# Hymba step on one Trainium2 core: the last head pair's keys and values stored from SBUF

## The chip, the cores and the metric

The kernel runs on one core of one Trainium2 chip. The metric is the device time of one execution in microseconds (us). In what follows PE is the matrix engine, DVE the vector engine, ACT the scalar engine, POOL is GpSimd and SP the engine that here only issues DMAs. ACT issues DMAs too. "The SP queue" and "the ACT queue" are the two DMA queues; in the profile they are q1 and q10.

## What is computed

One layer of a decoder, for 512 prompt tokens and 8 samples of 8 new tokens, with a cache of 2048 keys and values per sample:

```python
proj = jnp.einsum('btd,de->bte', x, w_in)                 # 1024 -> 4096
q, k, v, g_att, gb, gc, hh, g_conv = jnp.split(proj, ...)
o_att = _dilated_attention(q, k_all, v_all, offset)       # windows (128,1) (512,4) (2048,16)
att = o_att * jax.nn.silu(g_att)
u = gc * hh                                               # width-3 causal convolution of u
z = gb * y_conv * jax.nn.silu(g_conv)
out = jnp.einsum('bte,ed->btd', jnp.concatenate([att, z], axis=-1), w_out)
y = _layer_norm(DEEPNORM_ALPHA * x + out, ln_g, ln_b)
new_k = k_all[:, n_all - keep:]                           # the whole cache is an output again
new_v = v_all[:, n_all - keep:]
```

The last two lines matter here: the caches of keys and values are read, and nearly all of them must be written again as outputs. The host splits each cache into a part that the dilated windows use ("used") and one that they don't ("rest").

## The kernel before

All tensors are float32. Products of the two projections are made of three passes over a high and a low part of each operand (`x_hi`, `x_lo`, `w_hi`, `w_lo`). ACT makes a high part by a rounding copy, DVE the low part by a subtraction.

The input projection works through 32 weight tiles of 128 columns. Each tile from 2 on is loaded by SP into one of two slots of `w_raw` (512 KB, `load_w`, L311), rounded by ACT (`split_hi`, L510), subtracted by DVE (`split_lo`, L847) and multiplied by PE in two halves (`project`, L1239 to L1241, banks `pj_a` and `pj_b`). The tiles are taken in four rounds, one for a pair of heads; tiles 27 to 31 belong to the last round (`act_last_round`, `dve_last_round`, `pe_last_round`). Round by round the attention of a head pair stands between the projections: for the samples PE reads the used keys from `k_buf` in four pieces (L1402, `sample_scores`) and the used values from `v_buf` in ten half pieces, which are loaded two at a time (L1436, `sample_values`).

SP loads in a written order: weight tiles, four key pieces of 1280 KB per pair (L318, semaphores `k_in`), five value loads of 1024 KB per pair (L325, `v_in`). At the end it loads eight tiles of `w_out` into `wo_raw` (512 KB each, `load_wo`, L392). `wo_raw` lies over `k_buf` and other early buffers, so that the first four wait for `k_used`, PE's count of key pieces that it has read. ACT rounds them in `split_wo` (L689) and DVE subtracts (L1013). Later SP loads `ln_gb` (L428) and the residual rows `x_res` (L438), which lie over `v_buf` from the second tile of rows on.

The used and rest parts of the caches go to their outputs by 57 copies from HBM to HBM, each issued by ACT wherever `copy_next` stands in its written program (L539 rest, L548 values, L543 keys; 1024 KB, keys 1280 KB). Their order is: 24 copies of the rest, 17 of values, 16 of keys. Three more pieces of values (numbers 2, 3, 4 of the last pair, `STORED`) are stored from `v_buf` by SP (`store_values`, L420). All copies count on one semaphore, `copied`, and the three stores on `v_stored`; SP waits for both totals as its last act.

Behind the input projection stand the output projection (L1561 to L1595, five tiles of tokens) and the layer norm on DVE (L1186 to L1230). The last tile's rows are stored by SP (L458) and ACT (L837) in halves.

What an engine's program holds is executed in its order: a DMA whose semaphore isn't there yet holds up all that stands behind it on SP or on ACT.

Of the kernel before, what the change touches and what calls it, by code (L numbers as in the profile page):

```python
# [7 lines left out]
P = 128  # L8
# [21 lines left out]
NPAIR = DEC_BATCH // 2  # L30
# [11 lines left out]
K_PIECES = 4  # L42
# [3 lines left out]
V_LOADS = V_PIECES // 2  # L46
STORED = (2, 3, 4)
N_COPIES = 2 * REST_ROWS + NPAIR * (K_PIECES + V_LOADS) - len(STORED)
QT = SEQ // P
# [44 lines left out]
def layer_step(nc, d):  # L94

    with ExitStack() as ctx:
# [6 lines left out]
        def sem(name):  # L103
            return ctx.enter_context(nc.semaphore(name))
# [66 lines left out]
            sem("k_saved"), sem("v_saved"), sem("vn_saved"), sem("copied"), sem("conv_out"))  # L171
        v_stored = sem("v_stored")
        y_out = [sem(f"y_out{n}") for n in range(Y_SLOTS)]
# [132 lines left out]
        def _(sp):  # L306
# [88 lines left out]
            pieces = K_PIECES * (NPAIR - 1)  # L395
            sp.wait_ge(k_used, pieces + 1)
            load_wo(0)
            load_v(NPAIR - 1, 2)
            load_w(W_TILES - 1)
            sp.wait_ge(k_used, pieces + 2)  # L400
            load_wo(1)
            load_v(NPAIR - 1, 3)
            sp.wait_ge(k_used, pieces + 3)
            load_wo(2)
            load_v(NPAIR - 1, 4)
            sp.wait_ge(k_used, pieces + 4)
            load_wo(3)
            load_wo(4)
# [8 lines left out]
            def store_values(m):  # L417
                n = V_LOADS * (NPAIR - 1) + m
                sp.wait_ge(v_in[m], 16 * NPAIR)
                sp.dma_start(d["v_used_out"][n * P:(n + 1) * P, :], v_buf[:, m * 2048:(m + 1) * 2048])\  # L420
                    .then_inc(v_stored, 16)

            store_values(2)


# [10 lines left out]
            def load_res(t):  # L436
                rows = P if t != SAMPLE_AT else NS
                sp.dma_start(x_res[0:rows, t * 1024:(t + 1) * 1024], d["x_rows"][y_rows(t), :]).then_inc(res_in[t], 16)  # L438

# [23 lines left out]
            sp.wait_ge(copied, 16 * N_COPIES)  # L463
            sp.wait_ge(v_stored, 16 * len(STORED))

# [35 lines left out]
        def _(act):  # L501
# [44 lines left out]
            def copy_v(i, s):  # L546
                rows = slice((V_LOADS * i + s) * P, (V_LOADS * i + s + 1) * P)
                act.dma_start(short_runs(d["v_used_out"][rows, :]), short_runs(d["v_used"][rows, :]))\  # L548
                    .then_inc(copied, 16)

            copies = iter(range(N_COPIES))

            def copy_next():

                n = next(copies)
                if n < 2 * REST_ROWS:
                    copy_rest(n)
                elif n < N_COPIES - NPAIR * K_PIECES:
                    n -= 2 * REST_ROWS
                    copy_v(n // (V_LOADS), n % (V_LOADS))  # L560
                else:
                    n -= N_COPIES - NPAIR * K_PIECES
                    copy_k(n // K_PIECES, n % K_PIECES)
# [147 lines left out]
            def act_round(i):  # L711
# [42 lines left out]
                copy_q(i + 1)  # L754
                copy_next()
                split_hi(t0 + 8)
# [5 lines left out]
                split_k(i + 1, 1)  # L762
                copy_next()
                split_hi(t0 + 9)
                out_sample(i)

            def act_last_round(i):
                t0 = tile0(i)
                copy_c(i, 0)
                copy_next()  # L770
                out_sample_turned(i - 1)
                exp_prompt(i, 0)
                copy_c(i, 1)
                move_prompt(i, 0)
                exp_prompt(i, 1)
                split_hi(t0 + 2)
                move_prompt(i, 1)
# [31 lines left out]
                copy_next()  # L809
                copy_next()  # L810
                split_mix(2)
                copy_next()
                copy_next()
# [10 lines left out]
            for t in range(QT + 1):  # L824
# [7 lines left out]
                nc.scalar.activation(std[0:rows, :], rstd[0:rows, :], ACT.Sqrt).then_inc(ln_sqrt, 1)  # L832
                if t < 3:
                    copy_next()
# [882 lines left out]
```

## Time and profile before

| | us |
|---|---|
| median of 3 runs | 355.65 |
| the 3 runs | 355.65, 355.94, 352.95 |
| the profiled execution's own time | 352.72 |
| its span, first to last instruction | 350.9 |
| PE busy | 341.5 (97%) |
| DVE busy | 207.4 (59%) |
| ACT busy | 122.9 (35%) |
| DMA, mean rate | 402 GB/s over 141.03 MB |

The profile is of one execution. Its own time is 1.8 us above its span, and 2.9 us below the median of the runs. Idle time of an engine is read with what ended it; a DMA has a row at its issue and a time from there to its landing.

### The profile page before, as it was taken

To read this page: it belongs to the slowest core of one execution; us is meant where nothing else is said; L and a number is where in the kernel's file an instruction comes from. 1 tells how busy PE (TensorE), PEld (TensorE's weight loads), DVE (VectorE), ACT (ScalarE), POOL (GpSimd) and SP (SyncE) were. 2 spreads that over 40 slices of the span, in tenths; PEclk is the share of its full clock that TensorE was granted. 3 is DMA by queue.
4 is the path that set the end of the run, shared out by engine and by line. 5 is a ranking of instruction groups with operands and counts; after the bars stand their busy time and mean duration, and the time that the engine had idled before them with its cause. 6 is when DMAs were issued, how large, how long until landed. Compare 5 with 4: busy or idle time off the path is not lost.

```text
span 350.9 us, 7296 instructions
## 1 busy us (share of the span) xinstructions
PE 341.5 (97%) x3048; PEld 298.4 (85%) x3048; DVE 207.4 (59%) x397; ACT 122.9 (35%) x249; POOL 11.4 (3%) x28
## 2 busy tenths in 40 slices
PE   8999999999999999999999999999999999999991
PEld 6998888998889889988898899888889887888791
DVE  3744518955254657652546486524546699794874
ACT  5634324342244333422442425224442744310100
POOL 0010000000100000001000000010000000200000
PEclk9999999999999999999999999999999999999997
DMA  8999999999999999999999999999999999999995
GB/s 293 401 423 424 408 422 419 421 423 420 420 418 420 424 421 418 378 420 418 416 417 423 419 418 365 420 403 419 424 422 417 419 410 339 378 400 391 406 356 221
DMA packets 31570, 141.03 MB, mean 402 GB/s; under 512 B 3121, under 2 KB 3505, under 8 KB 26545
## 3 DMA queue, kind: packets, MB, share of 16 engines
q1 hardware_dynamic: 15890, 76.34, 53.4%
q10 hardware_dynamic: 15648, 64.23, 46.3%
q8 instruction: 24, 0.39, 0.4%
q14 instruction: 8, 0.07, 0.0%
HBM read 132.66 MB, written 71.86 MB: 583 GB/s over the span
## 4 chain that ended last, share of the span: by engine, by line
PE 81%; DMA 9%; DVE 6%; ACT 2%; issue 1%; ACTq 0%; DVEq 0%
PE pj_b L1239 9%; DMA w_raw<-in_w_tiles 9%; PE pj_b L1241 8%; PE pj_b L1240 8%; PE pj_a L1239 7%; PE pj_a L1240 6%; PE pj_a L1241 6%; PE sc L1436 4%; PE sc L1402 4%; PE px L1593 3%; PE px L1595 3%; PE px L1594 3%; PE po L1382 2%; PE pt L1368 2%; PE px L1350 2%; DVE rg L974 1%
## 5 line engine op out<-in xcount | busy, mean ns | idle before, releaser
L1239 PE MATMUL pj_b<-x_hi,w_hi 128*128 128x320 f32 x248 | 78.5, 316 | 0.3 <-DVE mix L990 0.3
L1240 PE MATMUL pj_b<-x_lo,w_hi 128*128 128x320 f32 x248 | 76.5, 308 | 0.0
L1241 PE MATMUL pj_b<-x_hi,w_lo 128*128 128x320 f32 x248 | 76.5, 308 | 0.0
L1239 PE MATMUL pj_a<-x_hi,w_hi 128*128 128x256 f32 (+1 forms) x248 | 71.6, 289 | 0.0
L1241 PE MATMUL pj_a<-x_hi,w_lo 128*128 128x256 f32 (+1 forms) x248 | 69.4, 280 | 0.0
L1240 PE MATMUL pj_a<-x_lo,w_hi 128*128 128x256 f32 (+1 forms) x248 | 69.4, 280 | 0.0
L847 DVE TENSOR_TENSOR w_lo<-w_raw,w_hi 128x1024 fp32r<-128x1024 f32 x30 | 36.7, 1223 | 27.5 <-ACT w_hi L510 27.5
L1239 PEld LDWEIGHTS pj_a<-x_hi,w_hi 128*128 128x128 f32 x248 | 46.9, 189 | 6.1 <-issue 5.5
L1239 PEld LDWEIGHTS pj_b<-x_hi,w_hi 128*128 128x128 f32 x248 | 46.5, 188 | 4.8 <-issue 3.6
L510 ACT CAST w_hi<-w_raw 128x1024 fp32r<-128x1024 f32 x30 | 31.4, 1045 | 46.0 <-PE pj_b L1241 28.6
L1241 PEld LDWEIGHTS pj_a<-x_hi,w_lo 128*128 128x128 f32 x248 | 46.7, 188 | 0.0
L1240 PEld LDWEIGHTS pj_a<-x_lo,w_hi 128*128 128x128 f32 x248 | 46.6, 188 | 0.0
L1240 PEld LDWEIGHTS pj_b<-x_lo,w_hi 128*128 128x128 f32 x248 | 46.5, 188 | 0.0
L1241 PEld LDWEIGHTS pj_b<-x_hi,w_lo 128*128 128x128 f32 x248 | 46.5, 188 | 0.0
L974 DVE RECIPROCAL rg<-rg 128x256 f32<-128x256 f32 (+1 forms) x16 | 31.3, 1954 | 0.6
L636 ACT ACTIVATE p_pr<-p_pr,stat 128x512 f32<-128x512 f32 (+3 forms) x32 | 17.7, 553 | 12.5 <-DVE stat L936 12.5
L1402 PE MATMUL sc<-k_buf,q_bd 128*32 128x320 f32 x256 | 20.3, 435 | 0.4 <-DVE stat L961 0.4
L936 DVE CUSTOM_DVE_ANT_0 p_pr<-px,mask_pr 128x512 f32<-128x512 f32 (+3 forms) x32 | 14.1, 487 | 9.7 <-PE px L1350 9.7
L1436 PE MATMUL sc<-v_buf,pt_s 128*32 128x256 f32 x320 | 19.3, 382 | 0.0
L642 ACT COPY pt_pr<-pt 128x384 f32<-128x384 f32 (+1 forms) x24 | 11.2, 517 | 15.3 <-PE pt L1368 15.3
L1436 PEld LDWEIGHTS sc<-v_buf,pt_s 128*32 128x32 f32 x320 | 9.4, 109 | 7.0 <-issue 1.8
L899 DVE COPY qk<-pj_b 128x320 f32<-128x320 f32 x4 | 2.0, 492 | 22.0 <-PE pj_b L1241 22.0
(175 smaller groups left out, 470.3 us busy)
## 6 DMA issues: line engine op xcount, KB each, us to landing
k_buf<-in_k_used SPq DMA_DIRECT2D x16, 1280.0 KB, 13.5
v_buf<-in_v_used SPq DMA_DIRECT2D x20, 1024.0 KB, 14.9
out_k_used_out<-in_k_used ACTq DMA_DIRECT2D x16, 1280.0 KB, 20.9
out_v_used_out<-in_v_used ACTq DMA_DIRECT2D x17, 1024.0 KB, 15.9
w_raw<-in_w_tiles SPq DMA_DIRECT2D x30, 512.0 KB, 9.7
out_k_rest_out<-in_k_rest ACTq DMA_DIRECT2D x12, 1024.0 KB, 14.6
out_v_rest_out<-in_v_rest ACTq DMA_DIRECT2D x12, 1024.0 KB, 16.4
wo_raw<-in_w_out SPq DMA_DIRECT2D x8, 512.0 KB, 13.7
```

What stands on the lines that cost most here:

```text
L510: nc.scalar.copy(w_hi[:, c], w_raw[:, c]).then_inc(w_hi_done, 1)
L636: nc.scalar.activation(p, p, ACT.Exp, bias=negmax_pr[:, st:st + 1], scale=-1.0, accum_out=sum_pr[:, st:st + 1]).then_inc(pr_exp, 1)
L642: nc.scalar.copy(pt_pr[:, e * SEQ:e * SEQ + step_width(s)], pt[e][:, 0:step_width(s)])\
L847: nc.vector.tensor_tensor(w_lo[:, c], w_raw[:, c], w_hi[:, c].bitcast(F32), ALU.subtract)\
L936: nc.vector.tensor_tensor_reduce(out=p_pr[:, e * SEQ + c0:e * SEQ + c1], in0=px[e][:, c0:c1], in1=mask_pr[:, SEQ - width(u):], scale=-SCAL ...
L974: nc.vector.reciprocal(rg[:, c], rg[:, c]).then_inc(g_step, 1)
L1239: nc.tensor.matmul(out, w_hi[:, w], x_hi[:, c], start=(k == 0), stop=False)
L1240: nc.tensor.matmul(out, w_hi[:, w], x_lo[:, c], start=False, stop=False)
L1241: return nc.tensor.matmul(out, w_lo[:, w], x_hi[:, c], start=False, stop=(k == KT - 1))
L1402: last = nc.tensor.matmul(sc[r * 32:r * 32 + 32, 0:K_COLS], q, k_buf[:, k0:k0 + K_COLS], start=(b == 0), stop=(b == 1 and not ends), skip_ ...
L1436: last = nc.tensor.matmul(sc[r * 32:r * 32 + 32, 0:2 * P], pt_s[:, t * P + r * 32:t * P + r * 32 + 32], v_buf[:, v0:v0 + 2 * P], start=(t ...
L1593: nc.tensor.matmul(out, m_hi, wo[:, hi], start=(n == 0), stop=False)
```

## The change

Every piece of the last pair's used keys and values now goes out from SBUF, where it lies anyway for the attention. Four stores of keys (`store_k`, 1280 KB each, from `k_buf`) are issued by ACT, each behind a wait that the piece has landed (`k_in`). Five stores of values, two of them new, are issued by SP. Six copies go: the four of those keys and the two of those values. The copies are 51 now. One call of `copy_next` is added early in the last round, two are taken out late in it, and two behind the layer norm's square roots; two calls in the third round and one at the start of the last become stores.

The single counts of stores are now one semaphore each. SP waits for `k_stored[c]` ahead of each of the loads of `w_out` that lie over the key piece, and for `v_stored[0]` or `v_stored[1]` ahead of the residual rows 1 to 4.

```diff
-STORED = (2, 3, 4)
-N_COPIES = 2 * REST_ROWS + NPAIR * (K_PIECES + V_LOADS) - len(STORED)
+N_COPIES = 2 * REST_ROWS + (NPAIR - 1) * (K_PIECES + V_LOADS)
...
+            sp.wait_ge(k_stored[0], 16)
             load_wo(0)
...
+            sp.wait_ge(k_stored[1], 16)
             load_wo(1)
...
+            sp.wait_ge(k_stored[2], 16)
             load_wo(2)
             load_v(NPAIR - 1, 4)
             sp.wait_ge(k_used, pieces + 4)
+            sp.wait_ge(k_stored[3], 16)
             load_wo(3)
...
+            store_values(0)
             store_values(2)
+            store_values(1)
...
             def load_res(t):
                 rows = P if t != SAMPLE_AT else NS
+                if t:
+                    sp.wait_ge(v_stored[(t - 1) // 2], 16)
...
+            def store_k(c):
+                n = K_PIECES * (NPAIR - 1) + c
+                act.wait_ge(k_in[c], 16 * NPAIR)
+                act.dma_start(d["k_used_out"][n * P:(n + 1) * P, :], k_buf[:, c * K_SLOT:(c + 1) * K_SLOT])\
+                    .then_inc(k_stored[c], 16)
...
             def act_last_round(i):
                 t0 = tile0(i)
                 copy_c(i, 0)
-                copy_next()
+                store_k(2)
                 out_sample_turned(i - 1)
                 exp_prompt(i, 0)
                 copy_c(i, 1)
+                copy_next()
                 move_prompt(i, 0)
                 exp_prompt(i, 1)
+                store_k(3)
                 split_hi(t0 + 2)
...
                 out_sample(i)
                 copy_next()
-                copy_next()
                 split_mix(2)
-                copy_next()
                 copy_next()
...
-                if t < 3:
+                if t < 1:
                     copy_next()
```

On ACT, at the turn from the third round to the last, these stood in a row before (`w_hi` is a weight tile's high part, `gcs` and `p_pr` are the convolution's gate and the prompt's scores):

```order
L543 DMA out_k_used_out<-in_k_used 16x16x1280
L685 COPY att_s<-pt 64x64 [waits so_turned]
L685 COPY att_s<-pt 64x64
L636 ACTIVATE p_pr,stat<-p_pr,stat 128x512 [waits pr_masked] x2
L649 COPY gcs<-pj_b 128x320 [waits vt_done,pj_b_done]
L642 COPY pt_pr<-pt 128x512 [waits pr_turned] x2
L636 ACTIVATE p_pr,stat<-p_pr,stat 128x384 [waits pr_masked] x2
L510 CAST w_hi<-w_raw 128x1024 [waits pj_b_done,w_in1]
```

and these stand there now:

```order
L563 DMA out_k_used_out<-k_buf 128x2560 [waits k_in2]
L700 COPY att_s<-pt 64x64 [waits so_turned]
L700 COPY att_s<-pt 64x64
L651 ACTIVATE p_pr,stat<-p_pr,stat 128x512 [waits pr_masked] x2
L664 COPY gcs<-pj_b 128x320 [waits vt_done,pj_b_done]
L552 DMA out_k_used_out<-in_k_used 16x16x1280
L657 COPY pt_pr<-pt 128x512 [waits pr_turned] x2
L651 ACTIVATE p_pr,stat<-p_pr,stat 128x384 [waits pr_masked] x2
L563 DMA out_k_used_out<-k_buf 128x2560 [waits k_in3]
L519 CAST w_hi<-w_raw 128x1024 [waits pj_b_done,w_in1]
```

The one copy has become a store of key piece 2, and two more DMAs of 1280 KB stand ahead of the tile's rounding: a copy, and the store of piece 3.

On SP, in the last round (`wo_raw` are the tiles of `w_out`), the difference is:

```order
-L392 DMA wo_raw<-in_w_out 128x1024 [waits k_used]
+L392 DMA wo_raw<-in_w_out 128x1024 [waits k_stored0,k_used]
 L325 DMA v_buf<-in_v_used 128x2048 [waits v_used]
 L311 DMA w_raw<-in_w_tiles 128x1024 [waits w_lo_done]
-L392 DMA wo_raw<-in_w_out 128x1024 [waits k_used]
+L392 DMA wo_raw<-in_w_out 128x1024 [waits k_stored1,k_used]
 L325 DMA v_buf<-in_v_used 128x2048 [waits v_used]
-L392 DMA wo_raw<-in_w_out 128x1024 [waits k_used]
+L392 DMA wo_raw<-in_w_out 128x1024 [waits k_stored2,k_used]
 L325 DMA v_buf<-in_v_used 128x2048 [waits v_used]
-L392 DMA wo_raw<-in_w_out 128x1024 [waits k_used]
+L392 DMA wo_raw<-in_w_out 128x1024 [waits k_stored3,k_used]
```

The loads stand where they stood; four of them have a second wait. The load of the last weight tile (L311) stands between the first and the second of these.

## Rows read from the trace of the kernel before

**Rows 1.** The page's first part and the rate of its 40 slices.
```profile
PE 341.5 (97%) x3048; PEld 298.4 (85%) x3048; DVE 207.4 (59%) x397; ACT 122.9 (35%) x249; POOL 11.4 (3%) x28
...
GB/s 293 401 423 424 408 422 419 421 423 420 420 418 420 424 421 418 378 420 418 416 417 423 419 418 365 420 403 419 424 422 417 419 410 339 378 400 391 406 356 221
```

**Rows 2.** Engines by stretch; last three: PE clock, DMA share, GB/s.
```profile
240.00:256.00 16.00, 16.00 (x166) 13.27 (x167) 8.81 (x24) 8.38 (x20) 0.00 (x0) 1.00 1.02 423
...
272.00:288.00 16.00, 15.74 (x145) 13.40 (x144) 12.67 (x18) 10.00 (x16) 0.00 (x0) 1.00 1.02 419
288.00:296.00 8.00, 8.00 (x76) 5.95 (x75) 7.93 (x9) 4.38 (x6) 0.00 (x0) 1.00 1.02 347
```

**Rows 3.** Timeline of ACT: start, us, instruction, idle before and releaser.
```profile
251.87 1.03 ACT L510 CAST w_hi<-w_raw 128x1024 fp32r<-128x1024 f32 x1
...
271.69 1.05 ACT L510 CAST w_hi<-w_raw 128x1024 fp32r<-128x1024 f32 x1 [5.03 <-PE pj_b L1241]
...
281.13 1.05 ACT L689 CAST wo<-wo_raw 128x1024 fp32r<-128x1024 f32 x1
...
284.22 0.38 ACT L654 ACTIVATE rg<-pj_a 128x256 f32<-128x256 f32 x1 [2.04 <-PE pj_a L1241]
...
291.72 1.05 ACT L689 CAST wo<-wo_raw 128x1024 fp32r<-128x1024 f32 x1
```

**Rows 4.** The chain that ended last, 270 to 292 us: start, us, what.
```profile
272.52 0.59 ACTq L543
...
274.20 1.89 ACT wo L689 x2
...
282.05 2.17 DVE rg L974
...
285.44 0.41 PE pj_b L1239
```

**Rows 5.** Timeline of SP: issues of the last weight tile and of a w_out tile.
```profile
254.19 0.33 SPq L311 DMA_DIRECT2D w_raw<-in_w_tiles  x1
...
264.21 5.07 SPq L392 DMA_DIRECT2D wo_raw<-in_w_out  x5
```

**Rows 6.** DMA issues, 254.1 to 254.5 us: KB, us to landing.
```profile
w_raw<-in_w_tiles SPq DMA_DIRECT2D x1, 512.0 KB, 10.0
```

**Rows 7.** DMA queues, 256 to 262 us: packets, MB, share of 16 engines.
```profile
q1 hardware_dynamic: 490, 2.47, 99.6%
...
q10 hardware_dynamic: 7, 0.02, 0.8%
```

**Rows 8.** DMA queues, 276 to 284 us.
```profile
q10 hardware_dynamic: 352, 1.72, 51.7%
q1 hardware_dynamic: 377, 1.67, 50.6%
```

**Rows 9.** DMA issues, 232.9 to 233.3 us (key piece 3).
```profile
k_buf<-in_k_used SPq DMA_DIRECT2D x1, 1280.0 KB, 14.3
```

**Rows 10.** DMA issues, 242.3 to 242.95 us (a key copy).
```profile
out_k_used_out<-in_k_used ACTq DMA_DIRECT2D x1, 1280.0 KB, 15.3
```

**Rows 11.** DMA issues, 264.2 to 264.5 us (w_out tile 3).
```profile
wo_raw<-in_w_out SPq DMA_DIRECT2D x1, 512.0 KB, 11.8
```

**Rows 12.** DMA issues, 268.85 to 269.2 us (w_out tile 7).
```profile
wo_raw<-in_w_out SPq DMA_DIRECT2D x1, 512.0 KB, 17.9
```

**Rows 13.** DMA issues, 292.5 to 292.8 us (residual rows 0).
```profile
x_res<-in_x_rows SPq DMA_DIRECT2D x1, 512.0 KB, 12.3
```

**Rows 14.** Timeline of DVE: the layer norm's first residual sum, and a wait later.
```profile
307.14 0.68 DVE L1186 SCALAR_TENSOR_TENSOR y_t<-x_res,px 128x512 f32<-128x512 f32 x1
...
325.08 0.69 DVE L1186 SCALAR_TENSOR_TENSOR y_t<-x_res,px 128x512 f32<-128x512 f32 x1 [4.00 <-PE px L1595]
```

**Rows 15.** DMA issues, 326.9 to 327.2 us (the last key copy, issued at 326.97).
```profile
out_k_used_out<-in_k_used ACTq DMA_DIRECT2D x1, 1280.0 KB, 22.2
```

**Rows 16.** DMA issues, 347.7 to 348 us (half of the last rows, issued at 347.76).
```profile
out_y<-y_t ACTq DMA_DIRECT2D x1, 256.0 KB, 2.7
```

More of the change, by code:

```diff
@@ L171, in layer_step @@
             sem("k_saved"), sem("v_saved"), sem("vn_saved"), sem("copied"), sem("conv_out"))
-        v_stored = sem("v_stored")
+        v_stored = [sem(f"v_stored{m}") for m in range(V_LOADS)]
+        k_stored = [sem(f"k_stored{c}") for c in range(K_PIECES)]
         y_out = [sem(f"y_out{n}") for n in range(Y_SLOTS)]
@@ L420, in store_values @@
                 sp.dma_start(d["v_used_out"][n * P:(n + 1) * P, :], v_buf[:, m * 2048:(m + 1) * 2048])\
-                    .then_inc(v_stored, 16)
+                    .then_inc(v_stored[m], 16)
+            store_values(0)
             store_values(2)
+            store_values(1)
             sp.wait_ge(s_pv, NPAIR)
@@ L463, in _ @@
             sp.wait_ge(copied, 16 * N_COPIES)
-            sp.wait_ge(v_stored, 16 * len(STORED))
+            for m in range(V_LOADS):
+                sp.wait_ge(v_stored[m], 16)
         @block.gpsimd
@@ L557, in copy_next @@
                     copy_rest(n)
-                elif n < N_COPIES - NPAIR * K_PIECES:
+                elif n < N_COPIES - (NPAIR - 1) * K_PIECES:
                     n -= 2 * REST_ROWS
@@ L561, in copy_next @@
                 else:
-                    n -= N_COPIES - NPAIR * K_PIECES
+                    n -= N_COPIES - (NPAIR - 1) * K_PIECES
                     copy_k(n // K_PIECES, n % K_PIECES)
@@ L754, in act_round @@
                 copy_q(i + 1)
-                copy_next()
+                if i < NPAIR - 2:
+                    copy_next()
+                else:
+                    store_k(0)
                 split_hi(t0 + 8)
@@ L762, in act_round @@
                 split_k(i + 1, 1)
-                copy_next()
+                if i < NPAIR - 2:
+                    copy_next()
+                else:
+                    store_k(1)
                 split_hi(t0 + 9)
@@ L773, in act_last_round @@
                 copy_c(i, 1)
+                copy_next()
                 move_prompt(i, 0)
                 exp_prompt(i, 1)
+                store_k(3)
                 split_hi(t0 + 2)
@@ L809, in act_last_round @@
                 copy_next()
-                copy_next()
                 split_mix(2)
-                copy_next()
                 copy_next()
```

## The prediction

> **What bounds the kernel now.** I read the page's first part first: PE is busy for 341.5 of 350.9 us [rows 1]. What is left is the start and the layer norm of the last tile, so a change can gain only there, and it loses whatever it makes PE wait. The clock was full (1.00) in all the stretches of [rows 2]. The rate of the 40 slices comes next: from the second slice on it stands near 420 GB/s [rows 1], and the table by stretch puts the DMA engines' share at 1.02 [rows 2]. So the DMA engines are full too, and a byte that is moved earlier on one queue makes a byte later on the other. That is the side from which this change is to be judged: it removes no work from PE, DVE or ACT.
>
> Then I looked for the loads that PE comes to need soonest. The last weight tile (31) is issued at 254.19 us [rows 5] and takes 10.0 us [rows 6], so it lands at 264.2. ACT rounds it at 271.69 and had been waiting for PE, not for the load [rows 3]: 7.5 us of slack. The chain that ended last says why that instruction matters. In the other rounds it runs along PE; from 272 to 285 us it runs over ACT (the queue's issue, two roundings of `w_out` from 274.20) and DVE (the gate's reciprocal until 284.2) to PE at 285.44 [rows 4]. An instruction of ACT that comes late at 271.69 delays all of this one for one, since nothing on that chain waits for anything else.
>
> **The change, part by part.** *Bytes.* A copy and a store move the same bytes through the DMA engines. In the stretch from 256 to 262 us the SP queue had them almost alone, with 2.47 MB in 6 us, or 412 GB/s [rows 7]; shared, they move 419 to 423 [rows 2]. I take 0.42 MB a us. Swapping a copy for a store of the same piece costs nothing by itself. What counts is when each is issued.
>
> *What ACT now issues ahead of the last weight tile.* Before, from 226.7 us until that tile landed, ACT issued three copies of values (1.05 MB each) and one of keys (1.31 MB). Now it issues, at the same places, stores of keys 0, 1 and 2 for the first, third and fourth, and then two more DMAs of 1.31 MB at about 249 and 252 us: a copy, and the store of keys 3, which stands just ahead of the rounding at 251.87 [rows 3]. The sum of what is added is 2 x 0.26 + 2 x 1.31 = 3.1 MB, which at 0.42 is 7.5 us. All of it is issued before the tile, and both queues have work, so all of it goes ahead of the tile or beside it. [Rows 7] show that it isn't filling a hole: the ACT queue had nothing left from 256 to 262 us, and the SP queue used the whole rate for these very loads.
>
> There is an echo. ACT's next copy is issued at 262.17 us, after which the tile needed 2 us only. A tile that is still 7.5 us off meets that copy, and where both queues have work they take turns packet by packet (352 to 377 packets in 8 us [rows 8]). So up to 1.31 MB more, 3.1 us, goes ahead. The tile lands between 264.2 + 7.5 = 271.7 and 264.2 + 10.6 = 274.8 us. Against 271.69 it is between 0.0 and 3.1 us late. I take 3.1, since the turns are nearly even and the copy's packets fit into the 7.5 us. If the ACT queue's larger packets (10 KB for a key store, 4 KB for a weight tile) give it more than its bytes, the tile comes still later; the price of this is bounded by one more of ACT's 1.31 MB, 3.1 us, so the term is 0 to 6.2, taken at **3.1 us**.
>
> *The tiles of `w_out`.* Each is behind the same bytes. Tile 3 is issued at 264.21 [rows 5] and lands 11.8 us later [rows 11], at 276.0; ACT takes it at 281.13 [rows 3]. By 10.6 us later it lands at 286.6, while ACT now wants it at 281.13 + 3.1 = 284.2. Its rounding takes 1.05 us, so it ends at 287.7. Behind it stands the gate's exponential of 284.22 [rows 3], now due at 287.3: 0.4 us late. Tile 7, issued at 268.85, lands 17.9 us later [rows 12] at 286.8, now at 297.4, wanted at 291.72 + 3.1 = 294.8 [rows 3]; DVE subtracts four of these in a row from there, and the last is needed some 3.5 us after ACT begins it, which hides it. Together **0.5 us**; from 0, if the echo is small, to 4, if every one of these is met by another copy of ACT.
>
> *The new waits on SP.* Key stores 0, 1 and 2 are issued at about 226.7, 240.1 and 242.4 us. The copy that stood at 242.4 took 15.3 us [rows 10]; by that the stores are there at 242, 255.4 and 257.7, against 244.75, 254.6 and 257.7 for the loads that wait. Store 3 is issued at 252 and is there at 267 to 268, so that tile 3 of `w_out` is issued some 3.5 us after 264.21, and tiles 4 to 7, queued behind it, follow. The SP queue still has older loads in it until 274 us, so this costs 0; without that cover it would be 3.5 us on tile 3, within the 4 above.
>
> *The new waits on ACT.* Key piece 3 was issued at 233.00 us and took 14.3 [rows 9], so it landed at 247.3; its store stands at 251.9, 4.6 us later, and behind it on ACT a weight tile's rounding. The pieces before have 4 us or more. The added bytes ahead of it are 0.26 MB, 0.6 us. Cost 0; up to 1 if a large store is just ahead.
>
> *Residual rows.* Two more stores of values, 2.1 MB or 5.0 us, are on SP ahead of `ln_gb` and `x_res`. Rows 0 landed at 292.5 + 12.3 = 304.8 [rows 13] and DVE took them at 307.14 [rows 14]. Behind tile 7 at 297.4 come three stores of 1.05 MB, at half the rate 15 us at most, so rows 0 land at 312 to 315 against 307.14 + 3.6 = 310.7: 1 to 4 us late. DVE waits 4.00 us for PE at 325.08 [rows 14], so it catches up. Cost 0, up to 3 if PE has to wait for the two sums.
>
> *The end.* The last key copy was issued at 326.97 and landed 22.2 us later, at 349.2 [rows 15]. The last rows of y landed at 347.76 + 2.7 = 350.5 [rows 16]. So in this execution the copies set nothing, and two fewer behind the layer norm gain 0. What they may gain in others is the second rival.
>
> **Sum.** 3.1 + 0.5 = 3.6 us on the profiled execution's own 352.72, which gives 356.3. That execution is 2.9 us under the median of the runs, 355.65, and nearest to the third of them. Carried to the median it is 355.65 + 3.6 = **359.3 us**. Its own range is 355.7 (both terms 0) to 362.3 (6.2 and 0.5).
>
> **The rivals.** *The tile is in time.* If the echo is small, it lands at 271.7 and ACT loses nothing: 355.6 us. For it: the margin is 7.5 us and the sum of bytes 7.5. Against it: the sum has no slack, and [rows 7] show no idle engine to take the bytes.
>
> *The end gets shorter.* Two of the three runs took 2.9 us more than the profiled one. If these are executions in which the copies landed after the last rows of y, then fewer copies at the end bring them back. For it: copies that run alone are slow. From 288 to 296 us the rate was 347 GB/s at the same share of 1.02 [rows 2], against 419 in the stretch before, so that a key copy alone costs 1.31 / 0.347 = 3.8 us in place of 3.1, and a store reads no HBM. Against it: the profile shows the last copy 1.3 us ahead of the end. It gives 355.65 - 2.9 = 352.7, less some tenths: 352.3 us. The Trainium skill has a rule for this ("HBM Reference", Specifications): a domain gives about 716 GB/s, reads and writes together being what a copy asks of it. By that rule a lone copy would run at half of 716, 358 GB/s, and the trace's 347 agrees. [...]
>
> *The loads starve.* If each late load lets more of ACT's copies pass, the tiles of `w_out` and the residual rows come late in turn: 6.2 for the weight tile and 2 for the rest, so 355.65 + 8.2 = 363.9 us. It decides once tile 31 lands more than 4 us after 271.69. Against it: while ACT waits it issues no copies, and the SP queue catches up.
>
> **Chances.** The forecast 0.40, the tile in time 0.24, the shorter end 0.19, the starved loads 0.17. About 1% (3.6 us) is what a measurement of this kernel can tell from no change. The forecast lies just at that line: I give 0.26 of its 0.40 to slower and 0.14 to the same. The starved loads are slower. Of the shorter end 0.12 is faster and 0.07 the same; the tile in time is the same. That makes faster 0.12, same 0.45, slower 0.43. The range goes from 352.6 to 363.9 us and leaves out about half of each outer case.
>
> **What would show it.** In the new trace the last `w_raw` load should take about 20 us to land in place of 10.0; ACT's rounding of tile 31 should wait for that DMA at 272 to 275 us, in place of waiting for PE; PE should show a wait of 1 to 3 us between 272 and 290. `w_out` tile 3 should land near 287. The copies should be done several us before the last rows of y. The prediction is wrong if the tile lands by 271.7, or if it lands late and PE doesn't wait, or if the copies turn out to have set the end.

## Result, and the profile after the change

The changed kernel is slower: 361.70 us, median of 4 runs (359.84 to 363.76), against 355.00 (352.95 to 355.94, 4 runs) for the kernel before. The ratio is 1.0182, with a 95% interval of 1.0135 to 1.0229. The profiled execution took 360.69 us, span 358.9, against 352.72 and 350.9.

The page of the changed kernel: busy time, the clock and the rate in 40 slices, and the bytes of HBM.

```profile
PE 344.0 (96%) x3048; PEld 299.7 (84%) x3048; DVE 208.2 (58%) x397; ACT 122.9 (34%) x249; POOL 13.1 (4%) x28
...
PEclk9999999999999999999999999999999999998998
...
GB/s 296 401 423 416 407 423 420 420 420 420 420 421 422 424 419 397 386 423 415 406 425 420 422 384 385 422 414 428 418 414 423 421 420 426 400 401 384 398 77 58
...
HBM read 125.32 MB, written 71.86 MB: 549 GB/s over the span
```

Against [rows 1], PE is busy only 2.5 us longer, in a span longer by 8.0. The reads of HBM are down from 132.66 MB on the page before, by the six pieces that are no longer copied; the writes are the same. The DMA engines, busy to the end before, have next to nothing to do in the last two slices (77 and 58 GB/s, against 356 and 221): the last copy landed at 344.28 us, 14 us before the last rows of y (358.43). So the change did shorten the DMA work at the end, where it buys nothing.

Where PE waits, by what it waited for (us in total, times, longest):

```profile
PE pt L1443 <- ACT pt_s L679: 2.1, 1, 2.1
PE px L1614 <- DVE y_t L1207: 2.1, 1, 2.1
PE pj_b L1260 <- DVE mix L1011: 1.5, 1, 1.5
...
PE pt L1614 <- DVE x_lo L1046: 0.4, 1, 0.4
```

To see when time is lost I laid PE's 3048 instructions of both traces side by side and took the difference of their starts. It rises by 0.5 us in the first 55 us, where both programs are the same; then by 2.2 at 277.8 us (the first of these waits), by 1.3 at 289 (the third), by 0.7 at 307.5 (the fourth), by 2.2 at 320.8 (the second), and by 1.7 just behind that wait. Sum: 8.6 us.

The loads behind these waits. ACT's timeline (what stands in brackets is the idle time before and what ended it), then DVE's, then two loads by their time to landing (windows at 254.5 and at 272.2 us):

```profile
275.70 1.04 ACT L519 CAST w_hi<-w_raw 128x1024 fp32r<-128x1024 f32 x1 [8.65 <-DMA w_raw<-in_w_tiles]
...
281.50 1.05 ACT L704 CAST wo<-wo_raw 128x1024 fp32r<-128x1024 f32 x1 [0.73 <-DMA wo_raw<-in_w_out]
283.07 0.44 ACT L669 ACTIVATE rg<-pj_b 128x320 f32<-128x320 f32 x1 [0.52 <-PE pj_b L1262]
...
288.59 1.04 ACT L704 CAST wo<-wo_raw 128x1024 fp32r<-128x1024 f32 x1 [4.43 <-DMA wo_raw<-in_w_out]
```

```profile
283.43 2.35 DVE L1034 TENSOR_TENSOR wo<-wo_raw,wo 128x1024 fp32r<-128x1024 f32 x2
285.70 0.32 DVE L993 TENSOR_SCALAR rg<-rg 128x320 f32<-128x320 f32 x1
...
288.90 0.49 DVE L1011 TENSOR_TENSOR mix<-pj_b,rg 128x320 f32<-128x320 f32 x1
```

```profile
w_raw<-in_w_tiles SPq DMA_DIRECT2D x1, 512.0 KB, 21.1
...
wo_raw<-in_w_out SPq DMA_DIRECT2D x1, 512.0 KB, 28.2
```

Tile 31 is issued at 254.57, 0.4 us later than before, and takes 21.1 us where [rows 6] have 10.0. In [rows 3] ACT had been waiting for PE at this place; now it waits for the tile, and rounds it 4.01 us later (275.70 against 271.69). PE's first and third wait both come from this. DVE's work behind the rounding has no gap in it that it didn't have before: the gate's product `mix<-pj_b,rg`, on which PE's third wait ends, starts at 288.90, and before at 284.90:

```profile
284.90 0.49 DVE L990 TENSOR_TENSOR mix<-pj_b,rg 128x320 f32<-128x320 f32 x1
```

So the lateness of tile 31 is passed on one for one, and by 291 us PE is 4.0 us late, the 0.5 of the start included. The tiles of `w_out` are late too: in [rows 3] ACT had no idle time ahead of tile 3, now a landing ends its wait there (288.59) and ahead of tile 2 (281.50). But they aren't what PE waits for at 289: the exponential behind tile 2 (283.07) waits for PE itself, and DVE, busy until then, takes it up at 285.70. `w_out` tile 7 is the one that costs. It takes 28.2 us against 17.9 [rows 12] and lands at 300.47, and the chain that ended last now runs through it, from store 3 of the keys:

```profile
251.52 15.97 DMA out_k_used_out<-k_buf
...
267.56 0.33 SPq L392
...
272.24 28.23 DMA wo_raw<-in_w_out
...
300.49 1.06 ACT wo L704
...
303.07 2.17 DVE rg L995
...
306.21 1.14 DVE x_lo L1046
...
307.49 0.47 PE pt L1614
```

The wait at 320.8, in PE's and DVE's timelines:

```profile
320.80 0.51 PE L1614 MATMUL px<-wo,x_hi 128*128 128x512 f32 x1 [2.07 <-DVE y_t L1207]
...
323.07 0.63 PE L1615 MATMUL px<-wo,x_hi 128*128 128x512 f32 x1
```

```profile
318.74 0.69 DVE L1207 SCALAR_TENSOR_TENSOR y_t<-x_res,px 128x512 f32<-128x512 f32 x1 [5.14 <-PE po L1616]
```

PE's third tile of tokens waits for the residual sums of the first, since it writes into their banks (L1573 of the changed kernel: `wait_ge(r_done, 2 * (t - 1))`). The DVE row names PE as what ended its 5.14 us of idle time. But of PE it only needs the first tile's products (`dve.wait_ge(o_done, 1)` here), which had been done for long: rows 0 of `x_res`, issued at 296.48 with 22.2 us to landing, were there at 318.65, 0.09 us before the row. So the releaser that a row names can be wrong; a run below names the DMA at this place. The loss of 1.7 us behind the wait is the clock: the granted clock was 0.62 over the next 4.5 us, which is 0.38 x 4.5 = 1.7. Engines by stretch, with the clock, the DMA share and GB/s as the last three:

```profile
320.80:325.30 4.50, 4.50 (x13) 3.55 (x14) 4.35 (x8) 0.20 (x1) 0.00 (x0) 0.62 1.01 419
```

### The profile page after: what moved, and what is told of

Read it like the earlier page. It is cut to its first block, busy times and chain, and to the rows that moved or that the text cites. A ratio compares the mean times of both kernels' runs of the same rounds, so it can differ in the third digit from the quotient of the medians.

```text
span 358.9 us, 7302 instructions
## 1 busy us (share of the span) xinstructions
PE 344.0 (96%) x3048; PEld 299.7 (84%) x3048; DVE 208.2 (58%) x397; ACT 122.9 (34%) x249; POOL 13.1 (4%) x28
## 4 chain that ended last, share of the span: by engine, by line
PE 69%; DMA 21%; DVE 5%; ACT 2%; SPq 1%; issue 1%; DVEq 0%; ACTq 0%
DMA w_raw<-in_w_tiles 8%; DMA wo_raw<-in_w_out 8%; PE pj_b L1260 8%; PE pj_b L1262 7%; PE pj_b L1261 7%; PE pj_a L1260 7%; PE pj_a L1261 6%; PE pj_a L1262 6%; DMA out_k_used_out<-k_buf 4%; PE sc L1457 4%; PE sc L1423 3%; PE px L1614 2%; PE px L1616 2%; PE px L1615 2%; PE px L1371 2%; PE pt L1389 2%
## 5 line engine op out<-in xcount | busy, mean ns | idle before, releaser
L1614 PE MATMUL px<-wo,x_hi 128*128 128x512 f32 (+1 forms) x40 | 15.5, 387 | 2.1 <-DVE y_t L1207 2.1
L1616 PE MATMUL px<-wo,x_lo 128*128 128x512 f32 (+1 forms) x40 | 15.5, 387 | 0.0
```

Source lines behind the costliest of these rows:

```text
L1614: nc.tensor.matmul(out, m_hi, wo[:, hi], start=(n == 0), stop=False)
L1616: last = nc.tensor.matmul(out, m_lo, wo[:, hi], start=False, stop=(n == KT - 1))
```

## The experiments

Each ratio is to runs of the kernel before that were made with it, with its 95% interval; "in the profile" means one profiled execution.

The loss can have two kinds of cause. Theory A: it is the place of bytes. ACT issues more megabytes ahead of the last weight tile, `w_out` and `x_res`, and these land late. Theory B: it is the stores, by their packets or by the waits that they put on SP and ACT.

**Copies in place of stores.** The keys are copied again, at the same places, and nothing waits for them.

```diff
-                act.wait_ge(k_in[c], 16 * NPAIR)
-                act.dma_start(d["k_used_out"][n * P:(n + 1) * P, :], k_buf[:, c * K_SLOT:(c + 1) * K_SLOT])\
-                    .then_inc(k_stored[c], 16)
+                act.dma_start(short_runs(d["k_used_out"][rows, :]), short_runs(d["k_used"][rows, :]))\
+                    .then_inc(copied, 16)
...
-            sp.wait_ge(k_stored[3], 16)
```

> The kernel after, but the four key pieces go out by copies from HBM, issued at the same places on ACT, with no wait of ACT for the piece and none of SP for a key store. Theory A (the place of the bytes on the queues makes the loss): the same bytes go ahead of the last weight tile, so its load still takes 18 to 22 us in place of 10.0, and the time stays within 1.5 us of the kernel after, 360 to 363 us (1.4 to 2.2% over before). Theory B (the new waits and the 10 KB packets of the key stores make it): the load takes 10 to 13 us and the time is within 2 us of before, 354 to 357.

Measured: 359.31 us, ratio 1.0132 (1.0080 to 1.0184). Tile 31 lands at 272.0, `w_out` tile 7 at 300.6, rows 0 at 318.2. Most of the loss is there without one store of keys or one wait on `k_stored`. The time is under the 360 to 363 us that I expected from theory A. The intervals of the two ratios overlap, so whether the stores add something isn't settled.

**Keys only, and values only.** The first stores the four key pieces and leaves values 0 and 1 to copies; the second stores all five value pieces and copies the keys.

```diff
+                if t < 3:
+                    copy_next()
...
-            store_values(0)
             store_values(2)
-            store_values(1)
```

```diff
-STORED = (2, 3, 4)
+STORED = (0, 1, 2, 3, 4)
...
+            store_values(0)
             store_values(2)
+            store_values(1)
```

> The key stores with their waits and the added early copy, values as before (three stores, two more copies behind the layer norm). Theory A: the last weight tile lands near 275 us and PE loses 3 to 4 us between 272 and 290, as after; residual rows 0 have 2.1 MB (5 us) less ahead of them and land near 312, so the wait of PE for the first residual sums (2.2 us) and the low clock behind it (1.7 us) go: 358 to 360 us. If instead the value stores make most of the loss, it is 354 to 356.

> Five value stores with their single waits, keys by copies at their old places, no added early copy. Theory A: the last weight tile lands at 264 to 266 us as before and PE waits for nothing up to 300; residual rows 0 come up to 5 us later than 304.8, near 310, and DVE takes them 3 us late, which PE doesn't see: 355 to 357 us. If the value stores make most of the loss by themselves, it is 359 to 361.

Measured: keys only 359.06 us, ratio 1.0127 (1.0095 to 1.0159), tile 31 at 275.6, tile 7 at 301.1. Values only 353.37, ratio 0.9976 (0.9947 to 1.0004), tile 31 at 271.3, tile 7 at 296.2. The half with the copy in between makes the loss. In the other half I missed the landing of tile 31, which came 7 us later than before, and the total, which I had at 355 to 357. With two copies of values fewer, the copies of keys, which are larger, begin two calls earlier, and so 0.5 MB more stand ahead of the tile. With the copy of 262 us, which a tile this late meets, that is 1.8 MB or 4.4 us; the rest of the 7 isn't explained. In the profile it cost PE nothing at tile 31, which was still 0.4 us ahead of 271.69, and 2.3 us at 305.0, behind tile 7.

**The added copy put at the end.**

```diff
                 copy_c(i, 1)
-                copy_next()
                 move_prompt(i, 0)
...
-                if t < 1:
+                if t < 2:
                     copy_next()
```

> The kernel after, but the copy that it adds early in the last round is issued behind the layer norm's second square root instead. Theory A: 1.31 MB (3.1 us, with its share of the echo up to 4.5) less ahead of the last weight tile, which lands at 271 to 272.5 us, so that PE's wait of 2.2 us near 275 goes and later loads come 3 to 4 us earlier: 356 to 358 us. Theory B (waits and packets of the key stores): no change from after, 360 to 363.

Measured: 355.67 us, ratio 1.0041 (1.0007 to 1.0076), a little under the 356 to 358 of theory A. This one copy gives back 1.4 of the 1.8%, 5 us. Tile 31 lands at 274.3 in the profiled execution (356.93 us), later than I had expected, and tile 7 at 298.4. That execution ends 3.8 us ahead of the profiled one of the changed kernel, and PE's starts say where most of it is: 1.3 us by 291 us (late by 2.7 in place of 4.0, again by as much as tile 31 is), 0.7 behind tile 7, and 1.5 because the clock didn't fall behind the wait for the sums. What is left there is mostly that wait: here the trace names the load.

```profile
316.84 0.69 DVE L1206 SCALAR_TENSOR_TENSOR y_t<-x_res,px 128x512 f32<-128x512 f32 x1 [7.10 <-DMA x_res<-in_x_rows]
```

**Order of SP's DMAs.** Residual rows first (R), weight tile 31 ahead of value piece 2 (W), and both.

```diff
             store_values(0)
-            store_values(2)
-            store_values(1)
...
             load_res(0)
+            store_values(1)
             load_res(1)
-            store_values(3)
+            store_values(2)
             load_res(2)
+            store_values(3)
             load_res(3)
```

```diff
-            load_v(NPAIR - 1, 2)
             load_w(W_TILES - 1)
+            load_v(NPAIR - 1, 2)
```

> The changed kernel with another order on SP's queue after the last w_out load: one store of values (piece 0) ahead of ln_gb and residual rows 0, and the stores of pieces 1, 2 and 3 each behind the next residual rows, where the changed kernel has three stores ahead of rows 0. Bytes, copies and everything before 273 us are the same. Theory A (the residual rows land too late for PE, and that wait also costs the stretch at half clock behind it): rows 0 land near 309 to 311 us in place of 318.65, PE doesn't wait for the two sums at 320.8 and its clock stays full there, and 3.9 us come back: about 357.8 us, ratio to before 1.006 to 1.012; the shifts of 2.2 and 1.3 us at 275 and 289 us stay. Theory B (the wait at 320.8 only takes what a later wait, of DVE for the layer norm, would take anyway): rows 0 land earlier as well, but the end moves by under 1 us: about 361, ratio 1.016 to 1.02.

> The changed kernel with the load of weight tile 31 issued ahead of the load of value piece 2, in place of behind it: 1.05 MB less ahead of the tile. Theory A (a wait that ends at a landing ends at the same time, however early PE comes to it): tile 31 lands 2.5 to 5 us earlier, at 271 to 273.2, and PE loses under 1 us at 275; but residual rows 0 still land near 318.6, so PE waits for the two sums at about 319 by 2 us more than before (4 in place of 2.2), and the time is that of the changed kernel within 1 us: 360.7 to 362.5. Theory B (the terms add up, each lost where its load is late): 2.2 to 3.5 us come back, about 358.8 us.

> The changed kernel with both orders: weight tile 31 ahead of value piece 2, and residual rows 0 ahead of all but one of the late stores. Theory A (landing times set the waits, and the last one hides the gain of the first): with the last wait gone the first gain shows too, so that this kernel is 2 to 3 us under the one with residual rows first alone: 354.8 to 356.5 us, ratio 1.000 to 1.005. Theory B (something else of the change costs time, as the bytes of the stores in the DMA engines or ACT's issues): it stays at 357 to 359, though both waits are gone from the trace.

Measured: R 360.70 us, ratio 1.0167 (1.0118 to 1.0217); W 361.69, 1.0196 (1.0134 to 1.0258); both 361.77, 1.0190 (1.0130 to 1.0250). None can be told from the changed kernel. PE's waits show why. R, then W, then both:

```profile
PE pt L1443 <- ACT pt_s L679: 3.6, 1, 3.6
PE pt L1614 <- DVE x_lo L1046: 1.8, 1, 1.8
```

```profile
PE pj_b L1260 <- DVE mix L1011: 3.6, 1, 3.6
PE px L1614 <- DVE y_t L1207: 1.4, 1, 1.4
...
PE pt L1443 <- ACT pt_s L679: 0.6, 1, 0.6
```

```profile
PE pj_b L1260 <- DVE mix L1011: 3.2, 1, 3.2
...
PE px L1614 <- DVE wo L1034: 1.3, 2, 1.1
PE pt L1443 <- ACT pt_s L679: 0.8, 1, 0.8
```

ACT's timeline with W:

```profile
285.38 1.05 ACT L704 CAST wo<-wo_raw 128x1024 fp32r<-128x1024 f32 x1 [5.34 <-DMA wo_raw<-in_w_out]
```

W does what it should at its own place (0.6 in place of 2.1 us, tile 31 at 273.9), and the time goes at the next one: `w_out` tile 2 lands at 285.4 in place of 281.5, ACT waits 5.34 us for it ahead of the exponential, DVE then waits for that exponential, and PE waits 3.6 us in place of 1.5. Behind this wait the granted clock was 0.62 over 4.5 us, and PE lost another 1.4 us; the wait for the sums (1.4) comes on top.

The profiles with a late tile 31 fall into two kinds. In five (changed, R, keys only, added copy at the end, and the same with R) PE is late at 291 us by as much as the tile is, against 271.69, within 0.1 us. In three (keys copied, W, both) tile 31 is only 0.3, 2.2 and 2.9 us late, but PE is 3.3 to 6.7: there `w_out` tile 2, which lands at 282.0 to 285.4, decides, with a low clock behind the wait.

With R the wait for the sums is gone (rows 0 at 311.4 in place of 318.7), yet in this execution tile 31 came at 277.8, 2.2 us later than in the profile of the changed kernel (0.6 of it there at its issue), though the program up to there is the same; PE was already late by more than the residual rows would have cost. Theory A's total for W held (360.7 to 362.5), though at another wait than it named; its 357.8 for R and 354.8 to 356.5 for both are refuted, and R came out at the rival's 361. In these runs the order within one queue only chose which load was late.

**Fewer copies between.** Values only, R, and ACT's call at about 240 us put behind the layer norm's square roots:

```diff
                 split_k(i + 1, 1)
-                copy_next()
+                if i < NPAIR - 2:
+                    copy_next()
...
-                if t < 1:
+                if t < 2:
                     copy_next()
```

> Key pieces copied as before; all five value pieces stored from SBUF (as in the run with values only, 353.4 us), residual rows first as above, and one of ACT's copies taken out at about 240 us and put behind the first tile's layer norm: 1.31 MB less ahead of the last weight tile and of the w_out tiles. By theory A (bytes ahead of a load that PE comes to need are what costs) tile 31 lands near 268 in place of 271.3, w_out tile 7 near 293 in place of 296.2, and the 2.2 us that PE loses at 302.8 in the run with values only falls to under 0.5: 351 to 352.5 us, ratio 0.990 to 0.995. Rival (the copy put at the end then sets the end, landing after the last rows of y at about 350): 353.5 us or more, with the last key copy landing after 350.

Measured: 353.31 us, ratio 0.9958 (0.9930 to 0.9985). Tile 31 at 264.6 and tile 7 at 287.1, earlier than expected, and PE loses 0.3 us after 270 us. The total is above the 351 to 352.5 that I expected from this: values only, with a tile 7 that is 9 us later, has nearly the same time (353.37). So below 6.3 MB fewer bytes gain nothing that shows. The rival doesn't fit either: the last copy landed at 349.4, ahead of 350.

**The added copy out, and R.**

> The changed kernel with the added copy put behind a layer norm (that run: 355.7 us, w_out tile 7 there at 298.4, PE losing 2.4 us at 313.9 for the residual sums) and with the residual rows ahead of the stores of values. Theory A (each of PE's waits ends a fixed time after a landing, and with tile 31 and tile 7 earlier nothing else takes the residual wait's place): the wait at 313.9 goes and 2.0 to 2.4 us come back: 353.2 to 354.2 us. Theory B (the order of the late DMAs is worth nothing, as with the changed kernel, where the rows came in time and the end moved by 1 us): 355 to 356 us.

Measured: ratio 1.0042 (1.0003 to 1.0080), that of the same kernel without R. Its ten runs spread from 352.75 to 360.42, with a median of 356.40; the ratio is of the seven shortest. The expected 353.2 to 354.2 is missed. The profile is of one of the three others (358.75): rows 0 were in time, tile 31 landed at 275.6 and tile 7 at 302.2. So R is worth nothing that shows, here too.

**Single causes, on the kernel before.** One copy moved from behind a layer norm to 249 us; and, in another kernel, the stores of values 3 and 4 ahead of `ln_gb` and `x_res`.

```diff
                 copy_c(i, 1)
+                copy_next()
                 move_prompt(i, 0)
...
-                if t < 3:
+                if t < 2:
                     copy_next()
```

```diff
             store_values(2)
+            store_values(3)
+            store_values(4)
```

> The kernel before with one change: one of ACT's copies of keys is issued at about 249 us in place of the third copy behind the layer norms. No stores are added. Theory A (a piece of 1.31 MB ahead of the last weight tile is what costs, by itself and by the next copy that it then meets): tile 31 lands at 268 to 271 in place of 264.2, w_out tile 7 at 290 to 295 in place of 286.8, both still in time, and the time is within 1 us of before: 354.5 to 356 us. Theory B (no margin at all: every early megabyte costs PE its 2.5 to 3 us): 357 to 358.5. If the copies at the end set the end in usual runs, 353.5 or less.

> The kernel before with the two stores of values 3 and 4 issued ahead of the layer norm's vectors and residual rows 0, in place of behind rows 1 and rows 4: 2.1 MB more ahead of rows 0 and nothing else. It measures the term for which I had taken 0. Theory A (PE can't begin a later tile's products before the residual sums, which come 2.15 us after the rows land, and a wait of 2 us also costs a stretch at half clock): rows 0 land at 311.5 to 316 in place of 304.8; PE waits at 313.9 wherever they land after 311.8, by as much as they are later, and the time rises by 1 to 4 us: 356 to 359. Theory B (my forecast's term: DVE catches up in its later wait of 4.00 us): within 0.5 us of before, 354.5 to 355.6 us, with no wait of PE for the sums.

Measured: 353.76 us, ratio 0.9994 (0.9969 to 1.0020), with tile 31 at 270.6 and tile 7 at 297.8; and 353.88 us, ratio 1.0007 (0.9984 to 1.0030). So the same 1.31 MB that cost 5 us in the changed kernel cost nothing that shows in the medians of the kernel before. There tile 31 has the slack for it: it lands ahead of 271.69. Tile 7 hasn't; it came later than the 290 to 295 that I expected. PE's timeline of this profiled execution (354.83 us) has a wait behind it, and PE ends 2.7 us later than in the profile of the kernel before (352.72 us). Here is the wait:

```profile
300.91 0.50 PE L1594 MATMUL px<-wo,x_hi 128*128 128x512 f32 x1 [1.77 <-DVE wo L1014]
```

What PE waits for in an execution of the kernel before near its median isn't known, so it stays open why the medians don't show these 2.7 us.

The second doesn't test what it was made for: rows 0 landed at 309.2, earlier than the 311.5 to 316 that I had reckoned, and not late for PE. So no run adds the wait for the sums by itself.

**Both stored, two copies fewer between.** As the kernel with the added copy out and R, and the call at 262 us moved to the end too.

```diff
                 split_hi(t0 + 3)
-                copy_next()
                 move_prompt(i, 2)
```

> As the kernel without the added copy and with the rows first, and ACT's copy at 262 us put behind a layer norm as well: keys and values stored from SBUF, two copies fewer between 249 and 263 us than in the changed kernel. Theory A (bytes ahead of tile 31 and of w_out are the whole cost; stores of keys, and the waits for them, cost nothing themselves): tile 31 lands at 266 to 271, tile 7 at 289 to 294, PE loses nothing after 270: 351.5 to 353 us. Theory B (the stores of keys cost by themselves, by SP's wait for store 3 or by the order of packets): PE still loses 1.3 us or more at 285, 353.5 us or more, above the kernel with values only and fewer copies between (353.3).

Measured: 352.70 us, ratio 0.9964 (0.9938 to 0.9990). Tile 31 at 269.7, tile 7 at 292.2. All three are as theory A had them; theory B had 353.5 us or more. The waits of PE that are left are of 1.3 us or less, the largest one early in the program, the same in the changed kernel. All four key stores with their waits are in it, the one ahead of `w_out` tile 3 with 2.6 us of waiting in place of 8.5:

```profile
PE sc L1286 <- DVE rg L861: 1.3, 1, 1.3
PE sc L1421 <- DVE stat L980: 0.7, 1, 0.7
PE pt L1387 <- DVE p_pr L970: 0.2, 1, 0.2
PE pj_b L1258 <- DVE mix L1009: 0.2, 1, 0.2
```

Theory B is left with nothing in this kernel; what it may have in the changed one is the difference to the kernel with keys copied, 0.5%, which the intervals don't tell from nothing. ACT is back where it was in [rows 3], waiting 5.03 us for PE ahead of tile 31:

```profile
272.25 1.05 ACT L519 CAST w_hi<-w_raw 128x1024 fp32r<-128x1024 f32 x1 [5.03 <-PE pj_b L1260]
```

**All runs together.** MB is what ACT issued from 225 to 266 us, copies and stores alike (1.31 a piece of keys, 1.05 of values); landings are of the profiled executions.

| kernel | MB | tile 31 | tile 7 | ratio |
|---|---|---|---|---|
| values only, fewer between, R | 4.98 | 264.6 | 287.1 | 0.9958 |
| before | 5.77 | 264.2 | 286.8 | 1 |
| before, stores ahead of rows | 5.77 | 265.6 | 290.4 | 1.0007 |
| both stored, two fewer, R | 6.29 | 269.7 | 292.2 | 0.9964 |
| values only | 6.29 | 271.3 | 296.2 | 0.9976 |
| before, one copy between | 7.08 | 270.6 | 297.8 | 0.9994 |
| added copy at the end | 7.60 | 274.3 | 298.4 | 1.0041 |
| the same with R | 7.60 | 275.6 | 302.2 | 1.0042 |
| keys only | 8.39 | 275.6 | 301.1 | 1.0127 |
| keys copied | 8.91 | 272.0 | 300.6 | 1.0132 |
| changed, R | 8.91 | 277.8 | 302.6 | 1.0167 |
| changed | 8.91 | 275.7 | 300.5 | 1.0182 |
| changed, both orders | 8.91 | 274.6 | 303.8 | 1.0190 |
| changed, W | 8.91 | 273.9 | 304.0 | 1.0196 |

Whatever is stored and in whichever order, the ratio follows the bytes. Up to 7.1 MB they cost nothing that can be told; from 7.6 to 8.9 MB the ratio rises by 0.9 to 1.5%, 3 to 5.5 us. The stretch from 225 to 266 us was chosen with the results at hand, so the table sums them up; what shows the cause are the pairs of kernels that differ by the place of one copy: changed against added copy at the end (1.0182, 1.0041), and that with R against two fewer with R (1.0042, 0.9964).

## Why the prediction was right, and where it was not

The forecast was 359.3 us, with 0.45 for the same and 0.43 for slower. Measured were 361.70, inside the range and inside the forecast's own range to 362.3. The mechanism is the forecast's: bytes moved ahead of loads on full DMA engines. The size was short. A rise of 3.6 us was forecast; it was 6.7 between the medians (361.70 and 355.00) and 8.0 between the two profiled executions. In the profile the terms were 3.5 us for tile 31 (3.1 forecast), 0.7 for `w_out` (0.5), 3.9 for the residual rows and the clock behind them (0), and 0.5 from the first 55 us, which no edit touches and which is between -0.2 and 1.1 in the other profiles. So two terms were right, and that the total still stayed inside the forecast's own range is in part luck: that range had no room set aside for the third.

*Bytes ahead of tile 31.* "The tile lands between 271.7 and 274.8 us": it landed at 275.68, 4.0 us after 271.69 where I took 3.1, inside the 0 to 6.2. "An instruction of ACT that comes late at 271.69 delays all of this one for one": so it was. PE lost 2.2 us at 277.8 and 1.3 at 289, and with the 0.5 from before that makes the 4.0. The echo is best seen in the kernel before with one copy between: 1.31 MB are 3.1 us, and tile 31 lands 6.4 us later, having met the copy of 262 us. With this copy out as well (added copy at the end against two fewer between) the tile lands at 269.7 in place of 274.3. In the changed kernel, taking 1.31 MB out gave back 5 us in the medians and 3.8 between the profiles, where 1.5 of it is a clock that didn't fall.

*`w_out`.* I took 0.5 us: 0.4 by the exponential of 284.22 behind tile 3, and tile 7 as hidden. Both readings were off. Tile 3 landed at 288.57, later than my 286.6, and the exponential behind it started 5.3 us later than before, but DVE took it up at 291.04, 4.0 us later like all its work there: cost 0. Tile 7 landed at 300.5 against my 297.4 and isn't hidden but next in line; the fourth wait measured 0.7. The size is about right in this profile. In the nine other profiles in which tile 7 landed after 296 us PE lost 1.5 to 3.0 us behind it in eight, and nothing in one (added copy at the end); in the four others, nothing.

*New waits on SP and ACT.* Taken at 0. SP did wait 8.5 us at L410, to 267.50, as forecast. With keys copied there is no such wait, and `w_out` tile 3 is issued at 263.94 in place of 267.56; yet it lands at 288.96 in place of 288.57, and tile 7 at 300.59 in place of 300.47. So in these profiles this wait moved no landing. The kernel with both stored and two copies fewer has all of these waits, this one shorter (2.6 us), at a ratio of 0.9964.

*Residual rows.* This is the step that failed: "1 to 4 us late. DVE waits 4.00 us for PE at 325.08, so it catches up. Cost 0." Rows 0 landed at 318.65, later than my 312 to 315, since each of the three stores took over 31 us from its issue behind the `w_out` tiles. And slack of DVE at 325 doesn't help: PE itself waits for the sums at 320.80. In all four profiles with that wait (changed, keys copied, added copy at the end, W) PE goes on 2.14 or 2.15 us after rows 0 land. In the changed kernel's profile the term measured 2.2 us and 1.7 of halved clock behind it, 3.9 in all. In usual runs it isn't shown to be that much: with R the median is 1.0 us lower, within the spread, and in its profile tile 31 and tile 7 had made PE 8.6 us late by 311 us. So the terms of a sum like mine aren't independent: PE goes on at the latest of what it waits for, and a wait that is taken away uncovers the next. For the sums the time from the landing is fixed, as said; behind tile 7 it was 7.0 to 8.8 us.

*The rivals.* The starved loads came as near as the forecast: the bound was 4 us late for tile 31, measured 3.99, the price 363.9. The measured time lies midway between the two, and that `w_out` tile 7 and the residual rows came late in turn is this rival's account. Its argument against, that SP catches up while ACT waits, is too weak: ACT's next copy goes out 0.13 us after the wait ends (275.83). The tile in time is refuted by the trace. The shorter end: the copies do end 14 us earlier, and PE's losses cover that. On a kernel that loses nothing it may be worth 1 to 2 us (0.9964 and 0.9958 above, with the last copy at 346.7 and 349.4 in the profiles). No profile of a run of the kernel before near its median was taken, so whether copies set the end there stays open.

## What to carry to other kernels

Where the DMA engines are full, as here, the place of a transfer is its cost: count the bytes that are issued ahead of each load that the busiest engine needs, and compare kernels by that before looking at who waits. Removing one late load's wait by reordering a queue moved the wait to the next load in all three versions that tried it; what helped was to take bytes out of that stretch and put them where nothing is loaded any more. Before you blame a late load for a wait, follow the waiting engine's input back: of the late tiles of `w_out` only those count that come later than what the vector engine was doing anyway. And ask of each late load which engine's next wait depends on it: slack of the vector engine somewhere behind says nothing if the matrix engine waits first.

Two versions are below both kernels, and can't be told apart: all pieces stored, residual rows first and two copies moved to the end (352.70 us, 0.9964 of before, 0.9938 to 0.9990), and values only with a copy fewer between and residual rows first (353.31 us, 0.9958, 0.9930 to 0.9985).

## What the runs showed of the hardware

- The clock behind a wait isn't the same each time. After the wait of 2.07 us at 320.80 the granted clock was 0.62 over 4.5 us (above), and matmuls started 0.43 us apart in place of 0.23. After a wait of 2.20 us at the same instruction, in the kernel with the added copy at the end, it stayed at 1.00; nor did it fall after 2.08 us at 277.77 in the changed kernel. Behind the six longer waits, 2.3 to 3.6 us (keys copied, keys only, R, W, both, and the added copy out with R), it fell each time, to 0.62 to 0.66 over 4.5 us; behind PE's waits of 1.1 to 1.8 us it never did. The same table for the kernel with the added copy at the end:

```profile
318.90:323.40 4.50, 4.50 (x20) 3.69 (x21) 4.36 (x8) 0.20 (x1) 0.00 (x0) 1.00 1.03 414
```

- Where loads and stores of SBUF stay in the queues, the rate stays up: from 288 to 296 us the changed kernel moves 422 GB/s, where the kernel before, with copies nearly alone, has 347 [rows 2].

```profile
288.00:296.00 8.00, 6.56 (x74) 5.20 (x75) 6.92 (x11) 3.88 (x6) 0.00 (x0) 1.00 1.03 422
```

- Landing times of one program differ from execution to execution: tile 31 by 2.2 us between two profiles whose programs are the same up to that point (changed and R; from issue to landing 21.1 and 22.6 us). A term of 2 us read from one profile needs the medians beside it.
- With ten or eleven DMAs of SP outstanding, issuing took longer: the three stores of values stand in SP's timeline with 6.17 us together, where the one at this place before took 0.43, with seven outstanding. With values only the three took 5.5 us, again with ten or eleven outstanding. That the number is the cause isn't tested.

```profile
273.34 6.17 SPq L424 DMA_DIRECT2D out_v_used_out<-v_buf  x3
```
